# The mixing stage of a two-layer network in another static order, and the transposed attention weights copied by ScalarE (two banks) and VectorE (one)

## The chip, the cores and the metric

One Trainium2 chip, one of its cores. The engines are TensorE (PE: matrix products and transposes), VectorE (DVE), ScalarE (ACT), GpSimd (POOL) and SyncE (SP, which issues most of the transfers). The metric is the device time of one execution, in microseconds; the kernel before is told by the median of its runs.

## The reference

Two layers over a sequence of 256 tokens of width 1024, all in float32. Each layer is a feed-forward block, a token-mixing block, a cross-attention to a memory of 256 tokens, and a second feed-forward block, each with a norm before and after. The token mixing projects the input to 2032 columns and feeds four mixers side by side:

```python
def _token_mixing(u, w_in, ...):
    proj = u @ w_in
    p_mla, p_nsa, p_fox, p_s5 = jnp.split(proj, ...)
    o_mla = _mla(...)      # causal attention over low-rank projections
    o_nsa = _nsa(...)      # compressed + selected + window attention, gated
    o_fox = _fox(...)      # causal attention with a forget gate
    o_s5 = _s5(...)        # state-space scan
    y = jnp.stack([o_mla, o_nsa, o_fox, o_s5], axis=2)
    y = _rmsnorm(y, group_g).reshape(B, S, MIX_WIDTH)
    return y @ w_out
```

The compressed branch of `_nsa` runs blocks of 32 keys and values through a small network (phi: 2048 to 256 to 64). The cross-attention needs keys and values of the normalized memory, `mem_n @ w_kv`, which depend on nothing in the layer.

## The kernel before

**Weights.** Each large weight is cut into units of 1 MB (128 x 2048). SyncE loads them one after the other into three slots; a load waits until the slot's former unit has been split by VectorE (L454). ScalarE copies the unit, in two halves, to a rounded high part (L666), VectorE subtracts it for the low part (L1141, called by `split_mid`). Products take three matmuls, high x high, high x low, low x high (`three`, L1677). ScalarE may overwrite a slot's high part when TensorE has done with the unit of three before (`unit_done`).

**The order of the work** is written out by hand, once for each engine; every engine runs its list in order and waits on semaphores. Between the two feed-forward blocks there are units 0 to 7 (input projection; 3 groups of two half units besides the first two), 8 and 9 (memory keys, `kv_half(0..1)`), 10 to 13 (phi), 14 to 19 (memory keys and values, `kv_half(2..7)`), 20 to 23 (output projection) and those of the cross-attention. The memory products fill TensorE's time between the steps of the mixers. Each has two halves of 24 matmuls of 256 columns; they go to PSUM banks 1, 1, 1, 3, 0, 1, 0, 1, emptied by ScalarE (`evac_kv`, L949 and L951). A half unit of the input projection (`group_half`) is 12 matmuls of 512 columns.

**Attention.** Four groups in the order 0 (MLA), 3 (fox), 1 and 2 (selected and window), each of four steps on TensorE: `scores` (16 matmuls), `probs_transposed` (12 transposes to banks 5, 6 and 7, L2002), `times_values` (24 matmuls). Between them VectorE takes the maximum (`attention_max`, L1430 and L1431), ScalarE the exponentials (`attention`, L932 and L935), then both copy the transposed weights from PSUM to SBUF: ScalarE bank 5 (L941), VectorE banks 6 and 7 (L1442). VectorE divides by the sum (`attention_out`, L1449).

**Steps around the change.** VectorE rotates the queries and keys of the second mixer together (L1404 to L1417). The memory tiles are made from a transposed copy in `zone`: x_hi by ScalarE (L966), x_lo by VectorE (`mem_lo`), in the order two tiles, `attention_max(0)`, six tiles. ScalarE has exponential, logarithm (L973) and tanh (L976), for which it loads function tables. The mixer outputs are normalized by group (`group_norm`), transposed (`mixer_transposed`, L2208), split into high and low (`mixer_hi`, L1053, `mixer_lo`) and multiplied with units 20 to 23 (`unit_rows`), whose sums lie in banks 0 to 3.

```python
                def attention_t(g):
                    act.wait_ge(*E.at("att_t", POS[g] + 1))
                    a.activation(probs_t[:, 0:512], bank(5), ACT.Copy).then_inc(sem["att_tc_act"], 1)
                def attention_copy(g):
                    dve.wait_ge(*E.at("att_t", POS[g] + 1))
                    v.tensor_copy(probs_t[:, 512:1536], bank(6, 2)).then_inc(sem["att_tc_dve"], 1)
```

## Time and profile before

| | us |
|---|---|
| median of 3 runs | 1329.68 (1329.3 to 1329.98) |
| the profiled execution | 1331.46 |
| its span | 1329.7 |
| TensorE, VectorE, ScalarE busy in it | 1284.1, 845.5, 683.3 |
| TensorE's mean granted clock | 0.983 |

Busy time is an average over stages. What matters is which engine the chain that ended last runs through, and, on that engine, where it stands still (the brackets behind a row of the timeline: how long it was idle and what released it) and where its clock is granted in part only (PEclk: 1.00 is 2.4 GHz, 0.50 is 1.2 GHz).

### The profile page before, as it was taken

The page shows a single profiled execution, that of the slowest core. Times are in us where ns is not written, and L with a number is a line of the kernel's source. Part 1 is how long each engine was busy: PE and PEld are TensorE (multiplying, and loading weights), DVE is VectorE, ACT ScalarE, POOL GpSimd, SP SyncE. Part 2 cuts the span into 40 slices and gives each one's busy share as a digit, 9 for nine tenths or more (in the row PEclk, how much of TensorE's full clock was granted, in tenths as well). Part 3 has the DMA queues.
Part 4 walks back from the last instruction along what each step waited for, and adds up shares of the span by engine and source line. Part 5 has one row for each costly group of instructions (what it writes and reads, how often), then busy time and mean ns, then how long its engine had stood idle before and what let it go on. Part 6 is the DMA issues. An engine that isn't in the chain of part 4 may idle for free.

```text
span 1329.7 us, 18613 instructions
## 1 busy us (share of the span) xinstructions
PE 1284.1 (97%) x6836; PEld 1096.8 (82%) x6836; DVE 845.5 (64%) x1173; ACT 683.3 (51%) x1113; POOL 235.8 (18%) x250
## 2 busy tenths in 40 slices
PE   7999999988999999999999999999899999999998
PEld 5887888778998978888878878887789888788886
DVE  5657857675666665555576577666766665755554
ACT  6455446474455554444464544554655454644443
POOL 1628900000002010000045296000000020100000
PEclk9999999998999999999999999999889999999999
DMA  9654543324334246555455555534143343555551
GB/s 345 247 189 158 204 175 127 142 96 159 127 127 167 102 170 247 189 189 189 158 181 188 188 185 189 190 112 158 64 159 127 128 171 112 215 188 189 189 189 64
DMA packets 32442, 222.65 MB, mean 167 GB/s; under 512 B 3584, under 2 KB 4096, under 8 KB 6784
## 3 DMA queue, kind: packets, MB, share of 16 engines
q1 hardware_dynamic: 30080, 209.28, 43.9%
q10 hardware_dynamic: 2304, 12.58, 2.5%
q8 instruction: 38, 0.62, 0.2%
q14 instruction: 20, 0.16, 0.0%
HBM read 219.75 MB, written 2.10 MB: 167 GB/s over the span
## 4 chain that ended last, share of the span: by engine, by line
PE 83%; DVE 7%; ACT 4%; issue 3%; DMA 1%; SPq 0%; POOL 0%; DVEq 0%; ACTq 0%; POOLq 0%
PE PS L1675 80%; DVE w_lo L1141 3%; PE PS L1790 1%; ACT w_hi L666 1%; DMA raw<-in_weights 1%; DVE x_lo L1144 1%; PE PS L2002 1%; ACT work L960 1%; DVE work L1144 0%; DVE work L1141 0%; DVE PS L1141 0%; DVE rope_t L1312 0%; ACT x_hi L714 0%; DVE h L1144 0%; DVE zone L1141 0%
## 5 line engine op out<-in xcount | busy, mean ns | idle before, releaser
L1141 DVE TENSOR_TENSOR w_lo<-raw,w_hi 128x1024 fp32r<-128x1024 f32 (+1 forms) x394 | 503.1, 1320 | 231.9 <-ACT w_hi L666 228.9
L666 ACT ACTIVATE w_hi<-raw 128x1024 fp32r<-128x1024 f32 x384 | 384.7, 1053 | 241.4 <-PE PS L1675 239.2
L1675 PE MATMUL PS<-w_hi,x_hi 128*128 128x512 f32 (+2 forms) x1104 | 426.9, 387 | 10.6 <-DVE x_lo L1144 5.3
L1675 PE MATMUL PS<-w_lo,x_hi 128*128 128x512 f32 (+2 forms) x1104 | 415.8, 377 | 0.0
L1675 PE MATMUL PS<-w_hi,x_lo 128*128 128x512 f32 (+2 forms) x1104 | 410.4, 378 | 0.0
L1675 PEld LDWEIGHTS PS<-w_hi,x_hi 128*128 128x128 f32 x1104 | 210.5, 191 | 53.2 <-DVE w_lo L1141 7.8
L1675 PEld LDWEIGHTS PS<-w_hi,x_lo 128*128 128x128 f32 x1104 | 210.0, 190 | 38.4
L1675 PEld LDWEIGHTS PS<-w_lo,x_hi 128*128 128x128 f32 x1104 | 211.0, 191 | 35.2 <-issue 0.5
L1675 PE MATMUL PS<-w_hi,hid_hi 128*128 128x512 f32 (+1 forms) x368 | 141.2, 386 | 0.0
L1675 PE MATMUL PS<-w_lo,hid_hi 128*128 128x512 f32 (+1 forms) x368 | 140.4, 385 | 0.0
L516 POOL TENSOR_SCALAR st<-st 128x1 f32<-128x1 f32 x32 | 20.3, 634 | 631.7 <-ACT proj L689 562.3
L727 ACT ACTIVATE work<-PS,st 128x256 f32<-128x256 f32 x88 | 41.8, 475 | 149.3 <-PE PS L1675 147.7
L1675 PE MATMUL PS<-w_hi,hid_lo 128*128 128x512 f32 (+1 forms) x368 | 111.2, 380 | 0.0
L1675 PE MATMUL PS<-x_hi,w_hi 128*128 128x256 f32 x288 | 87.9, 305 | 14.7 <-DVE x_lo L1144 7.0
L1675 PE MATMUL PS<-x_lo,w_hi 128*128 128x256 f32 x288 | 84.6, 294 | 0.0
L1675 PE MATMUL PS<-x_hi,w_lo 128*128 128x256 f32 x288 | 84.3, 293 | 0.0
L1144 DVE SCALAR_TENSOR_TENSOR work<-work,PS 128x256 f32<-128x256 f32 x88 | 36.7, 417 | 71.6 <-ACT work L727 71.6
L1675 PEld LDWEIGHTS PS<-w_hi,hid_hi 128*128 128x128 f32 (+1 forms) x368 | 67.3, 183 | 14.0
L1675 PEld LDWEIGHTS PS<-w_lo,hid_hi 128*128 128x128 f32 (+1 forms) x368 | 66.8, 182 | 13.6
L1675 PEld LDWEIGHTS PS<-w_hi,hid_lo 128*128 128x128 f32 (+1 forms) x368 | 66.5, 181 | 13.8
L1675 PEld LDWEIGHTS PS<-x_hi,w_hi 128*128 128x128 f32 x288 | 58.4, 203 | 17.8 <-issue 8.7
L1675 PEld LDWEIGHTS PS<-x_lo,w_hi 128*128 128x128 f32 x288 | 58.7, 204 | 0.1
(275 smaller groups left out, 1342.1 us busy)
## 6 DMA issues: line engine op xcount, KB each, us to landing
raw<-in_weights SPq DMA_DIRECT2D x194, 1024.0 KB, 4.7
pmat<-in_mats ACTq DMA_DIRECT2D x3, 1664.0 KB, 8.0
...
```

What stands on the lines that cost most here:

```text
L516: E.step(g.tensor_scalar(o, a, s1, s2, op0, op1))
L666: a.activation(w_hi[s][:, c_], raw[s][:, c_], ACT.Copy).then_inc(sem[hi_done[s]], 1)
L727: a.activation(f_th[:, t], bank(4 + t)[:, 0:UC], ACT.Tanh, scale=rstd[n][:, t:t + 1]).then_inc(sem["tanh_done"], 1)
L960: i = a.activation(y_to[32 * q:32 * q + 32, :, :, r], g_from[32 * r:32 * r + 32, q], ACT.Copy, scale=0.5)
L1141: return v.tensor_tensor(o, x_, y_, op)
L1144: return v.scalar_tensor_tensor(out=o, in0=x_, scalar=s_, in1=y_, op0=op0, op1=op1)
L1675: return t_.matmul(o, a_, b_, start=first, stop=last)
L1790: o = t_.transpose(bank(6)[:, j * S + t * P:j * S + (t + 1) * P], f_hid[:, t, j * P:(j + 1) * P], ident)
L2002: i = t_.transpose(bank(b)[:, hh * P:(hh + 1) * P], probs[:, at:at + P], ident)
```

## The change

The units between the input projection and the output projection are loaded in another order: keys and values 8, 9, 10, 12, 14, 15, 17, 19, phi 11, 13, 16, 18. All key/value units but the first go to bank 1. The lists of TensorE, ScalarE and VectorE are written anew: half of group (2,1) before the MLA transposes; scores of group 0 before the last half unit; the memory's x_hi in two halves, each when TensorE has done with the input tiles in the same place, and all x_lo before the maximum of group 0; the two rotations apart, that of the queries later; the compressed branch later; the output projection by token tile (`out_rows`), mixed with the last attention group and the compressed branch. ScalarE copies banks 5 and 6 of the transposed weights, VectorE bank 7. VectorE makes the key copy that ScalarE made (L982). The variance of the MLA norm is put before the second scan.

```diff
              [(I_FK, I_FV), (I_FV, I_FF)]]
 N_IN = 2 * len(IN_GROUPS)
 
-M_PHI = N_IN + 2
-KV_UNITS = [N_IN, N_IN + 1, *range(M_PHI + 4, M_PHI + 10)]
-KV_BANK = [1, 1, 1, 3, 0, 1, 0, 1]
-M_OUT = M_PHI + 10
+PHI_UNITS = [N_IN + i for i in (3, 5, 8, 10)]
+KV_UNITS = [N_IN + i for i in (0, 1, 2, 4, 6, 7, 9, 11)]
+KV_BANK = [0] + 7 * [1]
+M_OUT = N_IN + 12
 M_Q = M_OUT + 4
 M_O = M_Q + 4
 N_MID = M_O + 4
@@ -221,7 +221,7 @@
...
                 def attention_t(g):
                     act.wait_ge(*E.at("att_t", POS[g] + 1))
-                    a.activation(probs_t[:, 0:512], bank(5), ACT.Copy).then_inc(sem["att_tc_act"], 1)
+                    a.activation(probs_t[:, 0:1024], bank(5, 2), ACT.Copy).then_inc(sem["att_tc_act"], 1)
...
                 i.then_inc(sem["s5_sc_act"], 1)
+                act.wait_ge(*E.at("mem_in", 16))
+                for half in range(2):
+                    s, n, _ = mid(l, N_IN - 2 + half)
+                    act.wait_ge(*E.at(unit_done[s], n + 1))
+                    mem_hi(range(half * KT // 2, (half + 1) * KT // 2))
                 evac(3, 1)
-                act.wait_ge(*E.at("mem_in", 16))
-                for k in range(KT):
-                    a.activation(xh3[:, k], zone[:, 2048 + k * S:2048 + (k + 1) * S], ACT.Copy,
-                                     scale=pcol[:, C_MEM + k:C_MEM + k + 1]).then_inc(sem["x_hi_done"], 1)
-                attention(0)
-
-                act.wait_ge(*E.at("fox_x", 1))
-                a.activation(f_b2, f_a, ACT.Exp).then_inc(sem["fox_e"], 1)
-                act.wait_ge(*E.at("fox_e", 1))
-                a.activation(f_a, f_b2, ACT.Ln, bias=1.0).then_inc(sem["fox_ln"], 1)
+                split_mid(9)
...
-                act.wait_ge(*E.at("nsa_t", 1))
-                a.activation(kc2[0:HD, :], bank(6)[0:HD], ACT.Copy).then_inc(sem["nsa_kc"], 1)
-                a.activation(nsa_q[0:HD, :], bank(2, 2)[0:HD], ACT.Copy).then_inc(sem["nsa_tc_act"], 1)
+                attention(0)
+
+                act.wait_ge(*E.at("fox_x", 1))
+                a.activation(f_b2, f_a, ACT.Exp).then_inc(sem["fox_e"], 1)
+                act.wait_ge(*E.at("fox_e", 1))
+                a.activation(f_a, f_b2, ACT.Ln, bias=1.0).then_inc(sem["fox_ln"], 1)
                 split_mid(10)
+                evac_kv(0)
+                attention_t(0)
...
                 split_mid(11)
-                split_mid(13)
                 evac_kv(1)
+                split_mid(12)
                 act.wait_ge(*E.at("fox_cum", 1))
                 for hh in range(H):
                     i = a.activation(ka[HD:HD + 1, hh], bank(5)[32 * hh:32 * hh + 1, 0:S], ACT.Copy,
                                      scale=-1.0 / SCALE[3])
                 i.then_inc(sem["fox_nc"], 1)
+                evac_kv(2)
                 act.wait_ge(*E.at("fox_tq", 1))
                 a.activation(qk_a[0:HD, 0:H * S], bank(6, 2)[0:HD], ACT.Copy).then_inc(sem["fox_qt"], 1)
-                split_mid(12)
+                split_mid(13)
                 split_mid(14)
+                evac_kv(3)
                 attention(3)
 
                 split_mid(15)
-                evac_kv(2)
                 attention_t(3)
                 split_mid(16)
+                evac_kv(4)
+                split_mid(17)
+                act.wait_ge(*E.at("nsa_t", 2))
+                a.activation(nsa_q[0:HD, :], bank(6, 2)[0:HD], ACT.Copy).then_inc(sem["nsa_tc_act"], 1)
+                evac_kv(5)
+                attention(1)
+
+                split_mid(18)
+                attention_t(1)
+                split_mid(19)
+                evac_kv(6)
+                group_squares((0, 2), "att_out", 2)
+                split_mid(20)
+                act.wait_ge(*E.at("phi_h", 1))
+                act.wait_ge(*E.at("s5_out", 1))
+                for k in range(2):
+                    a.activation(s5_tiles[0][:, k], s_out[:, k], ACT.Copy).then_inc(sem["x_hi_done"], 1)
+                split_mid(21)
...
                 for n_ in range(2):
                     act.wait_ge(*E.at("grp_t", n_ + 1))
                     mixer_hi(MO_ORDER[2 * n_ + 2:2 * n_ + 4])
-                group_squares((1,), 4)
+                attention(2)
+                act.wait_ge(*E.at("cmp_x", 1))
+                a.activation(cp, cp, ACT.Exp).then_inc(sem["cmp_e"], 1)
+                attention_t(2)
+                act.wait_ge(*E.at("cmp_t", 1))
+                a.activation(probs_t[0:NC_CMP, 0:1024], bank(6, 2)[0:NC_CMP], ACT.Copy).then_inc(sem["cmp_tc"], 1)
+                group_squares((1,), "cmp_done", 1)
                 split_mid(23)
...
-                E.step(v.tensor_tensor_scan(s_tmp[3], kc2[:, :], s_tmp[2], 0.0, ALU.mult, ALU.add))
                 dve.wait_ge(*E.at("mla_sq", 1))
                 variance([(ss[N_MLA][:, 0:2], MLA_Q), (ss[N_MLA][:, 2:4], MLA_KV)])
+                E.step(v.tensor_tensor_scan(s_tmp[3], kc2[:, :], s_tmp[2], 0.0, ALU.mult, ALU.add))
...
                 def attention_copy(g):
                     dve.wait_ge(*E.at("att_t", POS[g] + 1))
-                    v.tensor_copy(probs_t[:, 512:1536], bank(6, 2)).then_inc(sem["att_tc_dve"], 1)
+                    v.tensor_copy(probs_t[:, 1024:1536], bank(7)).then_inc(sem["att_tc_dve"], 1)
...
+                mem_lo(range(KT))
                 attention_max(0)
-                mem_lo(range(2, KT))
                 split_mid(9)
...
-                attention_copy(0)
-
+                split_mid(10)
+                E.step(v.memset(zone[:, 7168:7168 + TT * P], 0.0))
+                dve.wait_ge(*E.at("fox_ln", 1))
+                tt(lf[:, :, 0:P:32], flog, f_a, ALU.subtract).then_inc(sem["fox_lf"], 1)
                 dve.wait_ge(*E.at("gate_th", 1))
                 E.step(v.tensor_scalar(gates, gates, 0.5, 0.5, ALU.mult, ALU.add))
 
                 attention_out(0)
                 split_mid(11)
-                split_mid(13)
+                split_mid(12)
...
                 dve.wait_ge(*E.at("fox_tk", 1))
                 v.tensor_copy(qk_a[0:HD, H * S:], bank(2, 2)[0:HD]).then_inc(sem["fox_kt"], 1)
-                split_mid(12)
                 dve.wait_ge(*E.at("s5_rstd_all", 1))
                 for k in range(2):
-                    i = stt(s_out[:, k], s_out[:, k], pcol[:, C_GRP + 6 + k:C_GRP + 7 + k], bank(1)[:, 0:S],
+                    i = stt(s_out[:, k], s_out[:, k], pcol[:, C_GRP + 6 + k:C_GRP + 7 + k], bank(4)[:, 0:S],
                             ALU.mult, ALU.mult)
                 i.then_inc(sem["s5_out"], 1)
+                dve.wait_ge(*E.at("proj_done", 7))
+                dve.wait_ge(*E.at("nsa_rope", 1))
+                nsa_rope(v3(pr3[:, :, I_NQ:I_KC], "p t (h d) -> p t h d", d=HD), H)
+                split_mid(13)
                 split_mid(14)
                 dve.wait_ge(*E.at("s5_var", 1))
                 attention_max(3)
 
                 split_mid(15)
                 attention_copy(3)
-                s, n, _ = mid(l, M_PHI + 3)
+                split_mid(16)
+                attention_out(3)
+                split_mid(17)
+                attention_max(1)
+
+                split_mid(18)
+                attention_copy(1)
+                split_mid(19)
+                s, n, _ = mid(l, PHI_UNITS[3])
                 dve.wait_ge(*E.at(unit_done[s], n + 1))
                 v.tensor_copy(phi_rows[0:2 * NC_CMP], bank(0)[0:2 * NC_CMP]).then_inc(sem["phi_h"], 1)
-                split_mid(16)
+                dve.wait_ge(*E.at("grp_sq", 1))
+                variance([(grp(ss, 0, 3, 2), 256)])
+                split_mid(20)
+                group_norm(0, 0, 3, 2)
+                dve.wait_ge(*E.at("x_hi_done", FILL[FI_MO] + 2))
+                for k in range(2):
+                    tt(s5_tiles[1][:, k], s_out[:, k], s5_tiles[0][:, k].bitcast(F32), ALU.subtract).then_inc(sem["x_split"], 1)
+                split_mid(21)
+                attention_out(1)
...
-                attention_out(3)
                 dve.wait_ge(*E.at("phi_th", 1))
                 stt(hx, hx2, 1.0, hx, ALU.add, ALU.mult).then_inc(sem["phi_hid"], 1)
-                split_mid(17)
...
+                split_mid(22)
+                attention_max(2)
+                mixer_lo(1)
+                mixer_lo(2)
...
-                group(3, 1)
+                group_half(3, 1, 0)
...
+                def out_rows(q, t, js):
+
+                    s, _, ns = mid(l, M_OUT + q)
+                    pe.wait_ge(*E.at(split_done[s], ns + 1))
+                    pe.wait_ge(*E.at("x_split", FILL[FI_MO] + 2 * q + 2))
+                    c_ = slice(t * P, (t + 1) * P)
+                    for j in js:
+                        ah, al = (x_[:, j, c_] for x_ in s5_tiles) if q == 0 else \
+                            (x_[:, MO_ORDER[2 * q + j], c_] for x_ in (xh3, xl3))
+                        o = [y_ps[:, t, n_ * 512:(n_ + 1) * 512] for n_ in range(2)]
+                        wh, wl = ([w[s][:, j * D + n_ * 512:j * D + (n_ + 1) * 512] for n_ in range(2)] for w in (w_hi, w_lo))
+                        for n_ in range(2):
+                            mm(o[n_], ah, wh[n_], q == 0 and j == 0, False)
+                            mm(o[n_], ah, wl[n_], False, False)
+                        for n_ in range(2):
+                            i = mm(o[n_], al, wh[n_], False, False)
+                    if t == 1 and j == 1:
+                        i.then_inc(sem[unit_done[s]], 1)
+
+                pe.wait_ge(*E.at("mla_qt", 1))
+                pe.wait_ge(*E.at("mla_kt", 1))
+                pe.wait_ge(*E.at("s5_yc", 1))
+                scores(0)
+                group_half(3, 1, 1)
+                pe.wait_ge(*E.at("proj_done", 8))
                 kv_half(0, 0)
...
                 kv_half(0, 1)
+                pe.wait_ge(*E.at("proj_done", 9))
+                kv_half(1, 0)
 
                 pe.wait_ge(s_con, 16)
                 pe.wait_ge(*E.at("s5_zt", 1))
                 pe.wait_ge(s_con, 16)
-                pe.wait_ge(*E.at("nsa_tc_act", 1))
-                pe.wait_ge(s_con, 16)
                 pe.wait_ge(*E.at("nsa_tc_dve", 1))
                 probs_transposed(0)
-                pe.wait_ge(*E.at("xkv_done", 1))
-                kv_half(1, 0)
+                kv_half(1, 1)
                 times_values(0)
-                pe.wait_ge(*E.at("blocks_done", 2))
-                phi_unit(M_PHI)
...
+                pe.wait_ge(*E.at("xkv_done", 2))
+                kv_half(2, 0)
+                pe.wait_ge(*E.at("blocks_done", 2))
+                pe.wait_ge(*E.at("xkv_done", 1))
+                phi_unit(0)
+                kv_half(2, 1)
 
                 fox_heads(I_FQ, 6, "fox_tq")
                 pe.wait_ge(s_con, 16)
                 pe.wait_ge(*E.at("att_out", 1))
                 fox_heads(I_FK, 2, "fox_tk")
-                phi_unit(M_PHI + 1)
-
                 pe.wait_ge(*E.at("s5_rstd", 1))
-                pe.wait_ge(*E.at("xkv_done", 2))
                 for t in range(TT):
-                    i = mm(bank(1)[:, t * P:(t + 1) * P], s5_r[:, t:t + 1].to_broadcast([P, P]), ident, True, True)
+                    i = mm(bank(4)[:, t * P:(t + 1) * P], s5_r[:, t:t + 1].to_broadcast([P, P]), ident, True, True)
...
+                pe.wait_ge(*E.at("xkv_done", 3))
+                kv_half(3, 0)
                 pe.wait_ge(*E.at("fox_one", 1))
                 pe.wait_ge(*E.at("fox_nc", 1))
                 pe.wait_ge(*E.at("fox_qt", 1))
                 pe.wait_ge(*E.at("fox_kt", 1))
+                pe.wait_ge(*E.at("s5_out", 1))
                 scores(3)
-
-                pe.wait_ge(*E.at("s5_out", 1))
-                kv_half(2, 0)
-                phi_unit(M_PHI + 2)
-                kv_half(2, 1)
+                kv_half(3, 1)
+                phi_unit(1)
+                pe.wait_ge(*E.at("xkv_done", 4))
+                kv_half(4, 0)
                 probs_transposed(3)
-                phi_unit(M_PHI + 3)
-                pe.wait_ge(*E.at("att_exp", 2))
-                kv_half(3, 0)
+                kv_half(4, 1)
                 times_values(3)
+                pe.wait_ge(s_con, 16)
+                pe.wait_ge(*E.at("nsa_rope", 2))
...
+                i.then_inc(sem["nsa_t"], 1)
+                pe.wait_ge(*E.at("xkv_done", 5))
+                kv_half(5, 0)
+                pe.wait_ge(*E.at("att_out", 2))
+                pe.wait_ge(*E.at("nsa_tc_act", 1))
+                scores(1)
+                kv_half(5, 1)
+                phi_unit(2)
+                pe.wait_ge(*E.at("xkv_done", 6))
+                kv_half(6, 0)
+                probs_transposed(1)
+                kv_half(6, 1)
+                phi_unit(3)
+                pe.wait_ge(*E.at("xkv_done", 7))
+                kv_half(7, 0)
+                pe.wait_ge(*E.at("nsa_v", 1))
+                times_values(1)
...
-                kv_half(3, 1)
-
+                kv_half(7, 1)
+                pe.wait_ge(*E.at("att_out", 3))
+                scores(2)
...
+
+                pe.wait_ge(s_con, 16)
+                pe.wait_ge(*E.at("grp_xn", 1))
+                mixer_transposed(MO_ORDER[2:4])
+                mixer_transposed(MO_ORDER[4:6])
+                pe.wait_ge(*E.at("xkv_done", 8))
+                out_rows(0, 0, range(2))
                 pe.wait_ge(*E.at("phi_c", 1))
...
+                out_rows(1, 0, range(2))
                 pe.wait_ge(s_con, 16)
                 pe.wait_ge(*E.at("cmp_x", 1))
-                probs_transposed(1)
-                kv_half(5, 1)
-                pe.wait_ge(*E.at("nsa_v", 1))
-                times_values(1)
+                pe.wait_ge(*E.at("x_split", FILL[FI_MO] + 6))
+                probs_transposed(2)
+                out_rows(0, 1, range(2))
+                times_values(2)
...
+                out_rows(1, 1, range(2))
+                pe.wait_ge(*E.at("att_out", 4))
                 pe.wait_ge(*E.at("cmp_tc", 1))
...
+                out_rows(2, 0, range(2))
+                out_rows(2, 1, [0])
                 pe.wait_ge(s_con, 16)
-                pe.wait_ge(*E.at("cmp_done", 1))
...
+                pe.wait_ge(*E.at("grp_xn", 2))
+                mixer_transposed(MO_ORDER[6:8])
+                out_rows(2, 1, [1])
+                s, _, ns = mid(l, M_OUT + 3)
+                pe.wait_ge(*E.at("x_split", FILL[FI_MO] + KT))
+                unit_rows(s, ns, [(xh3[:, k], xl3[:, k]) for k in MO_ORDER[6:8]], False, True)
                 pe.wait_ge(*E.at("x_split", FILL[FI_MO] + KT))
                 rows_transposed(2)
 
@@ -2340,13 +2350,17 @@
             u = u.reshape(KT, P, 2 * UC).transpose(1, 0, 2)
```

## Rows read from the trace of the kernel before

**Rows 1.** The page, part 1: busy us (share of the span) and instructions.

```profile
PE 1284.1 (97%) x6836; PEld 1096.8 (82%) x6836; DVE 845.5 (64%) x1173; ACT 683.3 (51%) x1113; POOL 235.8 (18%) x250
```

**Rows 2.** The page, part 4: the chain that ended last, by engine.

```profile
PE 83%; DVE 7%; ACT 4%; issue 3%; DMA 1%; SPq 0%; POOL 0%; DVEq 0%; ACTq 0%; POOLq 0%
```

**Rows 3.** Windows: stretch, length, busy us (instructions) by engine; PEclk; DMA share; GB/s.

```profile
247.30:413.80 166.50, 156.22 (x1039) 142.01 (x1039) 106.66 (x186) 86.23 (x162) 6.15 (x9) 0.94 0.35 127
...
902.60:1069.10 166.50, 156.23 (x1038) 142.06 (x1039) 106.65 (x186) 86.22 (x162) 6.15 (x9) 0.94 0.35 127
...
250.00:255.00 5.00, 5.00 (x19) 4.00 (x17) 4.15 (x10) 1.34 (x4) 0.00 (x0) 0.66 0.10 11
...
288.60:292.00 3.40, 3.40 (x17) 3.40 (x18) 3.40 (x7) 3.38 (x10) 0.00 (x0) 0.55 0.00 0
...
304.00:310.00 6.00, 6.00 (x42) 5.26 (x41) 3.33 (x7) 0.55 (x1) 0.00 (x0) 0.72 0.01 3
...
324.30:330.00 5.70, 5.70 (x30) 5.59 (x31) 3.21 (x6) 2.35 (x8) 0.00 (x0) 0.57 0.99 417
...
380.00:384.00 4.00, 4.00 (x24) 4.00 (x23) 2.62 (x5) 3.12 (x9) 0.00 (x0) 0.57 0.00 0
```

**Rows 4.** Timeline of PE, first layer: start, us, line, operation, count [idle before <-releaser].

```profile
242.12 0.40 PE L1675 MATMUL PS<-w_hi,x_lo 128*128 128x512 f32 x1
...
242.35 0.40 PE L1675 MATMUL PS<-w_hi,x_hi 128*128 128x512 f32 x1
...
249.64 0.40 PE L1953 MATMUL PS<-con,proj 128*96 128x128 f32 x2 [2.33 <-DVE proj L1141]
...
257.40 4.47 PE L1675 MATMUL PS<-pmat,nsa_q 96*128 96x384 f32 x12
...
288.60 0.58 PE L1675 MATMUL PS<-x_hi,w_hi 128*128 128x256 f32 x1 [3.02 <-DVE x_lo L1144]
...
299.07 0.38 PE L1675 MATMUL PS<-x_hi,w_hi 128*128 128x256 f32 x1 [0.78 <-ACT zone L949]
...
303.11 1.08 PE L1675 MATMUL PS<-v_mla,zone 128*128 128x65 f32 x8 [0.91 <-DVE zone L1442]
...
318.48 2.78 PE L1675 MATMUL PS<-qk_a 65*128 65x256 f32 x16
...
324.29 0.55 PE L1675 MATMUL PS<-x_hi,w_hi 128*128 128x256 f32 x1 [3.03 <-DVE w_lo L1141]
```

**Rows 5.** Timeline of DVE, first layer, same columns.

```profile
278.69 1.29 DVE L1141 TENSOR_TENSOR rope_t<-proj,con 128x512 f32<-128x512 f32 x2
...
280.02 0.76 DVE L1141 TENSOR_TENSOR proj<-rope_t 128x256 f32<-128x256 f32 x2
...
301.75 1.22 DVE L1442 COPY zone<-PS 128x1024 f32<-128x1024 f32 x1
...
316.89 1.21 DVE L1511 COPY qk_a<-PS 64x1024 f32<-64x1024 f32 x1
...
318.73 2.36 DVE L1141 TENSOR_TENSOR w_lo<-raw,w_hi 128x1024 fp32r<-128x1024 f32 x2 [0.63 <-ACT w_hi L666]
...
321.01 0.87 DVE L1144 SCALAR_TENSOR_TENSOR work<-work,pcol,PS 128x256 f32<-128x256 f32 x2
...
324.06 1.29 DVE L1141 TENSOR_TENSOR PS<-PS,con 128x512 f32<-128x512 f32 x2
```

**Rows 6.** Timeline of ACT, first layer and its FFN.

```profile
164.82 1.28 ACT L666 ACT_TABLE_LOAD   x1 [3.13 <-PE PS L1675]
...
295.05 1.01 ACT L983 ACTIVATE nsa_q<-PS 64x1024 f32<-64x1024 f32 x1
...
298.91 0.59 ACT L941 ACTIVATE zone<-PS 128x512 f32<-128x512 f32 x1
...
327.65 1.57 ACT L932 ACTIVATE zone<-PS,st 128x256 f32<-128x256 f32 x4 [6.11 <-DVE st L1141]
...
329.09 1.16 ACT L935 ACTIVATE zone<-PS,st 128x128 f32<-128x128 f32 x4
```

238 lines of the change are left out of this document (75 added, 163 removed).

## The prediction

> **What bounds the kernel now.** First the page: TensorE is busy 97% of the span, VectorE 64%, ScalarE 51% [rows 1], and the chain that ended last runs through TensorE for 83% [rows 2]. The change adds and removes no matrix work, so it can only touch the time in which TensorE stands still or runs at a lower clock between the third input group and the end of the output projection. I took that stretch from 247.3 us, where TensorE has ended group (2,0) and both orders still agree, to 413.8 us, the end of the last output unit. Of its 166.5 us TensorE is busy 156.2, so it waits 10.3, at a mean granted clock of 0.94; the second layer repeats it from 902.6 to 1069.1 with the same figures [rows 3]. Then the timeline, for where it waits: 2.33 us before the MLA transposes, 3.02 in the first key/value unit, 0.78 before the second, 0.91 before the first times-values, 3.03 before unit 14 [rows 4]; with 0.2 us of crumbs that is the 10.3. Last, windows behind each wait: the granted clock is 0.66 over 5 us, 0.55 over 3.4, 0.72 over 6, 0.57 over 5.7, and, with no wait ahead of it, 0.57 over 4 us at 380 [rows 3]. A share lost is one minus the clock, times the stretch: 1.70 + 1.53 + 1.68 + 2.45 + 1.72 = 9.1 us. **Losses are 10.3 + 9.1 = 19.4 us a layer**, 38.8 in all; without them the stretch is 147.1 us. That is what the change can win, and what new losses are counted against.
>
> **The unit costs.** A half unit of 512 columns is 12 matmuls, 0.23 us apart [rows 4]: 2.75 us. A half of a key/value unit is 24 matmuls, from 299.07 to 302.20 (303.11 less 0.91), of which some 0.2 is a tail that the next block overlaps: 2.9 us, 0.12 each [rows 4]. A phi unit is 16 such matmuls, 1.9 us. Scores are 2.8 us [rows 4]. VectorE's half of a weight split is 2.36 us for a unit [rows 5], ScalarE's two copies come ahead of it.
>
> **Part 1, the MLA transposes.** Before, they start at 249.64 after 2.33 us of waiting for VectorE's normalized projection, the clock is low behind it, and the MLA projections start at 257.40 [rows 4]. Afterwards the first half of group (2,1) is put in the gap: 247.3 + 2.75 = 250.05, by then the projection is there; transposes 0.6, second half 2.75, so the projections start at 253.4. Gain 4.0 us, which is 2.33 + 1.70. That VectorE computes the variance ahead of the second scan brings nothing by itself: the scan and the products still stand ahead of the normalization on its queue.
>
> **Part 2, memory tiles.** Before, six of eight x_lo tiles stand behind the softmax maximum of group 0 on VectorE, and TensorE waits 3.02 us for them [rows 4]. Afterwards ScalarE makes four x_hi tiles while TensorE does scores(0) and the last half unit (2.8 + 2.75 us), the other four when that half unit ends, VectorE follows tile by tile, and the maximum comes after all of them. TensorE starts tiles 0 to 3 at once (1.45 us of work) and meets the fifth some 0.4 us too early. Gain 3.0 + 1.5 less 0.4.
>
> **Part 3, group 0's probabilities.** The waits of 0.78 (one evacuation) and 0.91 (VectorE's copy) [rows 4] go: between the transposes and times_values stands a key/value half of 2.9 us, and the copy is shared anew. ScalarE now copies two banks, 1.01 us instead of 0.59 [rows 6]; VectorE one, about 0.7 instead of 1.22 [rows 5] (an estimate: half the columns and the fixed part). The two run side by side, so the pair is ready 0.2 us sooner, and 2.9 us of key/value matmuls or output rows cover it each time: this half of the change I cost at nothing; without the cover it would bring 0.2 us, four times a layer. Over a layer VectorE saves 2.1 us and ScalarE takes 1.7. Gain of the part 1.7 + 1.7 of clock.
>
> **Part 4, the order of units.** Before, the four phi units (1.9 us each on TensorE) come nearly in a row, while each needs 2.36 us of VectorE: TensorE outruns the splits and waits 3.03 us at unit 14 [rows 4, 5], with 2.45 us of low clock behind [rows 3]. Afterwards they are units 11, 13, 16, 18 with key/value units of 5.8 us between, and splits are taken in the order of loading. A slot's load follows the split of three units before, so the one issue that was early (13 ahead of 12) goes too; SyncE's queue has as many loads as before, merely of other units. Gain 3.0 + 2.45.
>
> **What comes new.** (a) Fox attention. Count from the end of the key transposes. VectorE: copy of the keys 1.21, s5 output 0.87, rotation of four heads 1.29 + 0.76, which was moved here, splits 13 and 14, 4.72, the maximum 324.06 to 327.65, 3.6: 12.5 us [rows 5, 6]. ScalarE then takes 2.6 for the exponentials (1.57 + 1.16, overlapping) [rows 6], and 1.28 for a table load, for now the last function before it is the logarithm: a load comes behind the wait, not under it, as the one at 164.82 that follows 3.13 us of waiting shows [rows 6]. Sum 16.3. TensorE from the same moment: 0.5 broadcast, key/value half 2.9, scores 2.8, half 2.9, phi 1.9, half 2.9: 13.9. It waits 2.4 us at probs_transposed(3), and the clock falls after it as after the others, 1.5 us. What stands behind is unit 14's second half and times_values. (b) In the output rows, the first mixer tiles' x_lo stand on VectorE behind split 22 and the maximum of group 2. From ScalarE's phi tanh: evacuation 0.6, first half of the split 1.0, then VectorE's 2.36, maximum 3.4, two tiles 0.87: 8.2 us [rows 5, 6]. TensorE over the same: the last 1.7 of scores(2), 0.7 of phi products, 0.9 of transposes, a half output unit 2.75, compressed scores 1.7: 7.7. Wait 0.5, behind it the probabilities of group 2. (c) The last unit needs the tiles of the group that is normed last: addition, squares, variance, GpSimd's power and the norm, some 3.3 us with their hand-overs, split 23 of 2.36 and two tiles of 0.87 make 6.6, against 5.9 of output rows and transposes: 0.7 us. The short operations in (b) and (c) are estimates after rows of like size, good to a microsecond either way. (d) The fall at 380 has no wait ahead of it, only scores and small products of 64 and 15 rows; such a stretch is still there (scores, phi output, transposes), so I keep one such fall, 1.7 us. (e) ScalarE waits about 6 us for unit 10 with the fox query copy and splits 13 and 14 behind it; the copy is still 1 us ahead of scores(3), so this costs nothing, and microsecond for microsecond beyond that.
>
> New losses: 0.4 + 2.4 + 0.5 + 0.7 + 1.5 + 1.7 = 7.2, with crumbs of 0.1 us 7.3. **Gain 19.4 - 7.3 = 12.1 us a layer, 24.2 in all.** The profiled execution took 1331.46 us (its span is 1329.7) and lies 1.8 above the median, so 1307.3 for it and 1305.5 for the median.
>
> For the two unseen sizes the bounds are: a new table load costs between nothing (hidden, or placed elsewhere) and 1.28 plus 1.5 of clock; I take it in full, since it sits on the longer path. A fall of the clock costs 0 to 2.45 us [rows 3], and there may be none or three.
>
> Where the load stands is the compiler's choice. Before, a load comes at the logarithm and, since a tanh follows, another at once, so no row shows what an exponential behind a logarithm needs; I place it at the first function of another kind, the exponentials of (a). The Trainium skill (ScalarE: Activation LUTs, Table sets) says otherwise: one shipped set has both the logarithm and the exponential, so that the one behind the other needs no second load. By that the sum would be the one of the rival "load elsewhere" below, 1302.5, and not 1305.5.
>
> **Rivals.** *Load elsewhere.* The exponentials need no load, and it comes ahead of the phi tanh, on the path to the compressed scores. In (a) 16.3 - 1.28 - 13.9 = 1.1 us of waiting stay, in (b) 0.5 + 1.28 = 1.8: the same sum in two shorter waits. After 0.78 us the clock kept its level, after 0.91 it fell [rows 3, 4]; if it keeps it here, 1.5 us a layer are saved: 1302.5. For it speaks the page named above, against it nothing but that no row shows it.
> *More places fall.* The new order has many seams with 1 us to spare, and ledger (d) may hold more than one fall. Two further falls (3.4) and waits of 2.5 us a layer halve the gain: 1317. For: five falls in 166 us before, one without a cause that I can name. Against: the three largest waits go surely.
> *All hidden.* The load is off the path and nothing falls without a wait: losses 2.8 us a layer, 1296.5. Against: VectorE's 12.5 us in (a) are counted from rows.
> *Slower: bank 1.* All key/value units but the first now use one bank, where three were used before, so each must wait until ScalarE has emptied it for the last. The one such wait before cost 0.78 [rows 4]; with a fall of 1.5 us behind each, six hand-overs cost 13.7 us a layer, more than the 12.1, and the kernel takes 1333. It decides from the point at which ScalarE reaches the evacuation later than TensorE the next unit. Against: between any two units stand a phi unit, transposes or times_values, 1.9 us or more, for a copy of 0.6; only at unit 19 is ScalarE busy ahead (a copy and a split), and has still 1.2 us.
> *No change.* The lists move work, but the waits that end last could come back in full elsewhere, 12 us of them; the stage behind depends on TensorE's end alone, so nothing swallows a gain there. 1329.7.
>
> **How the numbers follow.** The forecast 0.42, load elsewhere 0.2, more falls 0.2, all hidden 0.1, no change 0.03, bank 1 0.05. The range takes in the first four and somewhat over: 1295 to 1318. About 0.2% is what a measurement of this kernel can tell from no change; above it faster 0.92, same 0.03, slower 0.05.
>
> **What would show it.** Right: no wait before the MLA transposes; no wait over 0.6 us in the first key/value unit; none for w_lo in the middle; one wait of 1 to 2.5 us at the fox transposes of line 2002's operation, released by ScalarE; one or two low windows a layer instead of five; the stretch near 154 us. Wrong: waits of key/value units for ScalarE's evacuation, low clock in more than three places, or a stretch of over 160 us.

## The result, and the profile after

The changed kernel takes **1297.6 us** (median of 4 runs, 1297.27 to 1299.1) against 1329.83 beside it: ratio 0.9759 [0.9742, 0.9776], 32 us. The forecast was 1305.5 in a range from 1295 to 1318: the direction was right and so were the waits that go, the gain was a third larger than worked out, and the case that came nearest is the rival "all hidden" (1296.5), to which the prediction gave 0.1.

The profiled execution took 1297.27 us, its span is 1295.4, 34.3 less than before. Its page, parts 1 and 4 (the same lines as [rows 1, 2]):

```profile
PE 1266.7 (98%) x6836; PEld 1082.3 (84%) x6836; DVE 840.3 (65%) x1175; ACT 683.7 (53%) x1111; POOL 236.7 (18%) x250
...
PE 87%; DVE 6%; issue 3%; ACT 2%; DMA 1%; POOL 1%; SPq 0%; DVEq 0%; POOLq 0%; ACTq 0%
```

TensorE does the same 6836 instructions and is busy 17.4 us less, because it is not slowed. The rest of the gain is waiting. Windows after: the two stretches that answer to the first two of [rows 3], then four of the times of layer 1 at which the clock was low before (other work stands there now).

```profile
247.30:396.90 149.60, 147.36 (x1039) 133.92 (x1038) 104.06 (x187) 86.36 (x161) 5.46 (x8) 1.00 0.39 139
885.90:1035.50 149.60, 147.72 (x1040) 134.38 (x1039) 104.28 (x187) 86.48 (x162) 5.29 (x8) 1.00 0.40 141
250.00:255.00 5.00, 5.00 (x24) 3.73 (x22) 4.90 (x10) 3.81 (x7) 0.00 (x0) 1.00 0.07 18
...
288.60:292.00 3.40, 3.40 (x32) 3.40 (x31) 3.08 (x7) 2.91 (x5) 0.00 (x0) 1.00 0.45 188
304.00:310.00 6.00, 6.00 (x54) 6.00 (x53) 1.88 (x3) 3.35 (x4) 0.00 (x0) 1.00 0.46 188
324.30:330.00 5.70, 5.70 (x52) 5.70 (x52) 4.72 (x6) 5.53 (x7) 0.00 (x0) 1.00 0.52 172
```

The stretch was 166.5 us and is 149.6: 16.9 less, twice over 33.8 of the 34.3 us of span. TensorE now waits 149.60 - 147.36 = 2.24 us in it where it waited 10.3, and the clock column is 1.00 in both layers. So in layer 1 8.0 us came from waits and 8.9 from the clock, by which TensorE's busy time fell from 156.22 to 147.36; in layer 2 it was 8.4 and 8.5. (The windows of [rows 3] put the clock at 9.1, a little more than it cost.) **A good half of the gain is TensorE's clock**. Its timeline after, for the seams (the places where one block of work ends and TensorE may have to wait for the next) of [rows 4]:

```profile
249.73 0.38 PE L1951 MATMUL PS<-con,proj 128*96 128x128 f32 x2
...
253.14 4.47 PE L1671 MATMUL PS<-pmat,nsa_q 96*128 96x384 f32 x12
...
278.18 0.28 PE L1671 MATMUL PS<-x_hi,w_hi 128*128 128x256 f32 x1
...
322.90 1.50 PE L2000 MATMUL PS<-con,zone 128*128 128x128 f32 x12 [1.30 <-ACT zone L933]
...
367.07 1.95 PE L1671 MATMUL PS<-rope_t,nsa_q 64*128 64x15 f32 x16
...
391.29 0.50 PE L1671 MATMUL PS<-w_hi,x_hi 128*128 128x512 f32 x1 [0.94 <-DVE x_lo L1146]
```

No bracket stands behind the MLA transposes (249.73), the first key/value unit (278.18) or the compressed scores (367.07). Two waits are left: 1.30 us at the fox transposes, released by ScalarE's exponentials, and 0.94 for the last unit's x_lo (in layer 2 it is 0.6). What stands ahead of the first, on VectorE and then on ScalarE:

```profile
308.12 1.22 DVE L1517 COPY qk_a<-PS 64x1024 f32<-64x1024 f32 x1 [5.50 <-PE PS L2050]
309.26 0.85 DVE L1146 SCALAR_TENSOR_TENSOR work<-work,pcol,PS 128x256 f32<-128x256 f32 x2
310.04 1.28 DVE L1143 TENSOR_TENSOR rope_t<-proj,con 128x512 f32<-128x512 f32 x2
311.36 0.76 DVE L1143 TENSOR_TENSOR proj<-rope_t 128x256 f32<-128x256 f32 x2
312.03 4.62 DVE L1143 TENSOR_TENSOR w_lo<-raw,w_hi 128x1024 fp32r<-128x1024 f32 x4
316.57 1.29 DVE L1143 TENSOR_TENSOR PS<-PS,con 128x512 f32<-128x512 f32 x2
...
319.95 0.17 DVE L1143 TENSOR_TENSOR st<-st 128x8 f32<-128x8 f32 x1
```

```profile
316.93 0.60 ACT L947 ACTIVATE zone<-PS 128x512 f32<-128x512 f32 x1 [4.87 <-PE PS L1671]
317.54 1.28 ACT L930 ACT_TABLE_LOAD   x1
320.16 1.57 ACT L930 ACTIVATE zone<-PS,st 128x256 f32<-128x256 f32 x4 [1.33 <-DVE st L1143]
321.60 1.16 ACT L933 ACTIVATE zone<-PS,st 128x128 f32<-128x128 f32 x4
```

VectorE is 12.0 us from the key copy to the last small operation (12.5 forecast), the exponentials 2.6 (2.6 forecast). The table load is where the prediction put it, at the exponentials behind the logarithm, but it ran at 317.54, **while** ScalarE was still waiting for the maximum: the 1.33 us in the bracket come after the load, and its 1.28 us cost nothing.

Of the signs that the prediction named, these came: no wait before the MLA transposes, none in the first key/value unit, none for w_lo in the middle, and one of 1.30 us at the fox transposes. Two did not: there is no low window at all where one or two were expected, and the stretch is 149.6 us and not 154.

### The profile page after: what moved, and what is told of

Its sections match the earlier page's. It is cut to its first block, busy times and chain, and to the rows that moved or that the text cites. A ratio compares the mean times of both kernels' runs of the same rounds, so it can differ in the third digit from the quotient of the medians.

```text
span 1295.4 us, 18623 instructions
## 1 busy us (share of the span) xinstructions
PE 1266.7 (98%) x6836; PEld 1082.3 (84%) x6836; DVE 840.3 (65%) x1175; ACT 683.7 (53%) x1111; POOL 236.7 (18%) x250
## 4 chain that ended last, share of the span: by engine, by line
PE 87%; DVE 6%; issue 3%; ACT 2%; DMA 1%; POOL 1%; SPq 0%; DVEq 0%; POOLq 0%; ACTq 0%
PE PS L1671 82%; DVE w_lo L1143 3%; PE PS L1786 1%; DMA raw<-in_weights 1%; PE PS L2000 1%; DVE x_lo L1146 1%; DVE work L1146 0%; ACT w_hi L666 0%; DVE PS L1143 0%; DVE rope_t L1314 0%; ACT x_hi L714 0%; DVE h L1146 0%; PE PS L1812 0%; PE PS L2050 0%; PE PS L2259 0%
## 5 line engine op out<-in xcount | busy, mean ns | idle before, releaser
L1671 PE MATMUL PS<-x_hi,w_hi 128*128 128x256 f32 x288 | 84.0, 292 | 1.0 <-DVE x_lo L1146 0.9
L1671 PE MATMUL PS<-x_lo,w_hi 128*128 128x256 f32 x288 | 81.4, 283 | 0.0
L1671 PE MATMUL PS<-x_hi,w_lo 128*128 128x256 f32 x288 | 81.4, 283 | 0.0
L1671 PEld LDWEIGHTS PS<-w_hi,hid_lo 128*128 128x128 f32 (+1 forms) x368 | 66.5, 181 | 13.9
L1671 PEld LDWEIGHTS PS<-w_hi,hid_hi 128*128 128x128 f32 (+1 forms) x368 | 66.5, 181 | 13.6
L1671 PEld LDWEIGHTS PS<-x_hi,w_hi 128*128 128x128 f32 x288 | 55.0, 191 | 2.4 <-issue 1.8
L1671 PEld LDWEIGHTS PS<-x_lo,w_hi 128*128 128x128 f32 x288 | 55.1, 191 | 0.1
```

Source lines behind the costliest of these rows:

```text
L1671: return t_.matmul(o, a_, b_, start=first, stop=last)
```

## The experiments

Two families: kernels a... are the changed kernel with one thing undone, moved or added, kernels b... are the kernel before with one part of the change, or nothing, put in. Times stand beside the kernel before on the same chip: 1330.82 us for a1 to a4, 1330.12 for b1 to b4, 1330.86 for a5 to a7 and b5. Theory, as on record in the prediction: the gain is the waits and the low clock of the four parts, the sharing of the copies is worth nothing.

### a1: the sharing of the copies undone

```diff
-a.activation(probs_t[:, 0:1024], bank(5, 2), ACT.Copy)...
+a.activation(probs_t[:, 0:512], bank(5), ACT.Copy)...
-v.tensor_copy(probs_t[:, 1024:1536], bank(7))...
+v.tensor_copy(probs_t[:, 512:1536], bank(6, 2))...
```

> The kernel after, with the sharing of the transposed weights undone: ScalarE copies bank 5 (0.6 us), VectorE banks 6 and 7 (1.22 us). My theory: every copy lies under 2.9 us of key/value matmuls or output rows, so it changes nothing: 1297.6 within 0.15% (1295.7 to 1299.5), and no new wait of TensorE before times_values. Rival: VectorE's queue is what the wait at the fox transposes hangs on, and 0.5 us more on it for each group moves later steps: up to 0.5 us for each of four groups in two layers, 1301.6.

Measured: 1298.21 us (1297.45 to 1298.44), ratio 0.9762 [0.9743, 0.9782]; the waits are the same two, 1.3 and 0.9. The sharing of the copies, which the title names, makes 0.6 us between the medians, which the runs can't tell from nothing. The pieces are as costed: ScalarE's two banks take 1.03 us where one took 0.59, VectorE's one takes 0.68 where two took 1.22, and 2.9 us of matmuls cover either.

### a2: a second wait ahead of the load

```diff
 act.wait_ge(*E.at("att_max", POS[g] + 1))
+act.wait_ge(*E.at("att_s", POS[g] + 1))
```

> The kernel after, with a second wait (already met) between the wait for the maximum and the first exponential of every group. Theory A: a wait that stands alone next to an activation is carried by the activation itself, so the table load in front of it runs while ScalarE waits; with two waits the load comes behind the first, as in the loop of the feed-forward block (wait, load, activation). Then the load falls on the path: the exponentials start 1.3 us later, TensorE's wait at the fox transposes grows from 1.30 to 2.6 us, and the time by 2.6 us to 1300.2; if the clock falls behind the longer wait, by another 1.5 us a layer, 1303.2. Rival B: the load's place does not hang on the waits: no change, 1297.6.

Measured: 1297.99 us (1296.62 to 1302.24), ratio 0.9767 [0.9739, 0.9795]. ScalarE's timeline of a2:

```profile
318.93 1.28 ACT L931 ACT_TABLE_LOAD   x1
321.54 1.57 ACT L931 ACTIVATE zone<-PS,st 128x256 f32<-128x256 f32 x4 [1.33 <-DVE st L1144]
```

The load still ran ahead of both waits and TensorE's wait was still 1.3: the edit did not do what it was made for, and the theory that a second wait ahead of the exponentials puts the load behind the first fell. What does put it there is shown by a6.

### a3: part 1 undone

```diff
-                group_half(2, 1, 0)
...
-                group_half(2, 1, 1)
+                group(2, 1)
```

> The kernel after, with part 1 undone: the whole group (2,1) after the MLA transposes. Theory: the wait of 2.33 us comes back in each layer, and with it the low clock over some 3.4 us (1.7): 4.0 us a layer, 1305.6. Rival: slack behind it (VectorE, ScalarE ahead of the later steps) takes up part of the shift, under 2.3 us a layer, below 1302.2. Rival 2: the wait comes back but the clock holds, as it did behind 1.30 us in the kernel after: 4.7 us in all, 1302.3.

Measured: 1304.92 us (1303.76 to 1306.55), ratio 0.9815 [0.9794, 0.9837], 7.3 more than the changed kernel. TensorE's timeline of a3, and its windows behind the wait in both layers:

```profile
248.73 0.40 PE L1949 MATMUL PS<-con,proj 128*96 128x128 f32 x2 [2.27 <-DVE proj L1143]
```

```profile
248.00:254.00 6.00, 5.27 (x20) 4.32 (x21) 5.24 (x12) 1.26 (x4) 0.00 (x0) 0.72 0.03 5
889.50:895.50 6.00, 4.24 (x15) 3.64 (x16) 5.93 (x11) 1.56 (x5) 0.83 (x2) 0.72 0.00 0
```

Wait and fall are both back, 2.3 + 6 x 0.28 = 1.7 in each layer: 8.0 us by this count for the 7.3 measured. Part 1 is settled, at the 4.0 a layer that it was given less a little.

### b1: part 1 alone, in the kernel before

```diff
                 group(2, 0)
+                group_half(2, 1, 0)
...
-                group(2, 1)
+                group_half(2, 1, 1)
```

> The kernel before with part 1 alone: the first half of group (2,1) ahead of the MLA transposes. Theory: 2.33 us of waiting and 1.7 of low clock go in each layer, and what follows moves with it: 1329.8 - 8.0 = 1321.8. Rival: the later steps wait for ScalarE and VectorE, and less than half arrives at the end: over 1325.8.

Measured: 1322.82 us (1322.23 to 1324.35), ratio 0.9951 [0.9933, 0.997]: 7.3 us less, the same amount from the other side. The waits of 3.0, 3.0 and 0.9 stay, and that of 0.78 shrinks to 0.4. Windows of b1, all the low ones of the first mixer:

```profile
282.00:290.00 8.00, 5.78 (x27) 5.49 (x28) 6.83 (x13) 6.51 (x15) 0.00 (x0) 0.57 0.10 15
316.00:324.00 8.00, 4.97 (x25) 4.87 (x24) 6.38 (x10) 1.89 (x6) 0.00 (x0) 0.57 0.87 340
374.00:380.00 6.00, 6.00 (x38) 5.93 (x38) 4.16 (x6) 4.29 (x10) 0.00 (x0) 0.72 0.01 3
```

The fall behind the removed wait is gone and so is the one that stood at 304, but those behind the two waits of 3.0 are longer than before, and the mean granted clock of b1's runs is 0.984 to 0.987 (before: mostly 0.983 and 0.984). Waits explain some 5.3 of the 7.3 us, so the clock gave back about 2 and not the 3.4 that the theory had.

### b2: part 2 alone

```diff
-                mem_lo(range(2))
+                mem_lo(range(KT))
                 attention_max(0)
-                mem_lo(range(2, KT))
```

> The kernel before with part 2 alone, in its simplest form: all eight x_lo tiles ahead of the maximum of group 0. Theory: the wait of 3.02 us shrinks to under 0.5 and the low clock behind it goes, but the maximum, the exponentials and all that hangs on them come 2.5 us later, and TensorE waits for them at the transposes of group 0 instead: part of the 4.5 us a layer comes back, 1322 to 1328. Rival: nothing is lost behind, 1320.8.

Measured: 1334.95 us (1332.28 to 1337.27), ratio 1.0046 [1.003, 1.0063]: **slower** by 0.3 to 0.6%, which neither theory had. TensorE's timeline of b2:

```profile
291.53 1.89 PE L2071 MATMUL PS<-con,proj 128*64 128x128 f32 x8 [5.47 <-ACT st L971]
```

The 3.02 us wait of the key/value unit is gone, and 5.5 us stand in front of the transposes of the second mixer's queries. These write to banks 2 and 3, where scores(0) lie until the exponentials have read them, and those follow the maximum, which six tiles now hold up. The changed kernel escapes this because it makes those transposes much later and in other banks. Part 2 is not a gain by itself but one half of a pair.

### a7: part 2 undone, in the changed kernel

```diff
-                mem_lo(range(KT))
+                mem_lo(range(2))
                 attention_max(0)
+                mem_lo(range(2, KT))
```

> The changed kernel with VectorE's old order of the memory tiles: two tiles, attention_max(0), then the other six, everything else as in the changed kernel. Theory (making all eight ahead of the maxima is what took away the 3.02 us wait of the first key and value unit): that unit, which starts at 278.2 us without a wait, needs the third tile only after the 3.4 us of the maxima, so TensorE waits 2 to 3 us in each layer: 1297.6 + 2 x 2.5 = 1302.6 us, plus 0 to 1.5 a layer for a clock fall, 1301 to 1306. Rival (in the new order the tiles are early enough anyway, because the work ahead of them shrank): no wait, 1297.6 us.

Measured: 1303.86 us (1301.94 to 1305.54), ratio 0.98 [0.9786, 0.9813], 6.3 more. TensorE's timeline of a7, and its windows behind the wait in layer 1 and in layer 2:

```profile
281.73 0.39 PE L1672 MATMUL PS<-x_hi,w_hi 128*128 128x256 f32 x1 [1.74 <-DVE x_lo L1146]
```

```profile
282.00:286.00 4.00, 4.00 (x21) 3.92 (x21) 3.92 (x7) 1.64 (x2) 0.00 (x0) 0.57 0.01 4
919.00:925.00 6.00, 4.26 (x26) 3.66 (x25) 5.87 (x13) 4.99 (x12) 0.63 (x1) 1.00 0.00 0
```

The wait is back behind the second tile, 1.7 us in each layer: shorter than the 2 to 3 of the expectation, but the rival (tiles early enough anyway) fell. In layer 1 a fall of 4 x 0.43 = 1.7 us follows it, in layer 2 none does. Same wait, same program, two outcomes. The waits and the fall make 5.1 of the 6.3 us; 0.9 more lie ahead of the mixer, since TensorE reaches the unit at 279.11 in this profile and at 278.18 in that of the changed kernel. The other 0.3 us are not assigned.

### b3: a phi unit ahead of the key/value half

```diff
+                phi_unit(M_PHI + 2)
                 pe.wait_ge(*E.at("s5_out", 1))
                 kv_half(2, 0)
-                phi_unit(M_PHI + 2)
```

> The kernel before with one swap on TensorE: the third phi unit (12), whose split is done by then, ahead of the first half of unit 14. Theory: the wait of 3.03 us is the ring of three slots - unit 14 may only be split when phi unit 11 is through, and between them TensorE has 3.3 us of work where the split takes 6.8 - so 1.9 us of it are filled, about 1.1 us stay, and the low clock of 2.45 us behind it goes or shrinks: 1329.8 - 3.8 - (0 to 4.9) = 1321 to 1326. Rival: the phi unit itself must wait as long: 1329.8.

Measured: 1317.68 us (1315.74 to 1324.16), ratio 0.9926 [0.99, 0.9951], 12.4 us less than before, more than either theory gave. The wait for unit 14 went from 3.03 to 1.1 us, while two others grew (to 1.2 and 0.5), so waits explain some 2 us. The rest is the clock. Windows of b3, with the five stretches of [rows 3] and the only low one of both mixers:

```profile
250.00:255.00 5.00, 5.00 (x24) 4.12 (x23) 4.73 (x10) 3.21 (x5) 0.00 (x0) 1.00 0.18 28
288.60:292.00 3.40, 3.40 (x32) 3.39 (x31) 3.19 (x5) 3.34 (x6) 0.00 (x0) 1.00 0.22 34
...
895.00:901.00 6.00, 4.66 (x17) 4.01 (x18) 5.82 (x13) 1.19 (x3) 0.92 (x2) 0.72 0.00 0
```

The waits of 2.4 and 3.0 us before 250 and 288 are there, and the clock did not fall behind them in layer 1. The edit comes after both. Yet it can hardly be chance alone: the mean granted clock of b3's six runs is 0.998 three times (1315.7 to 1316.2 us), 0.994 once (1319.2) and 0.988 twice (1322.8 and 1324.2), while the 18 runs of the kernel before on the same chip have 0.981 to 0.990. So the 12.4 us are a median over runs with and without most of the falls, the two at 0.988 are those that fit the expectation of 1321 to 1326, and how an edit can act on a stretch ahead of it stays **open**.

### b4: the fall at 380

```diff
+                pe.wait_ge(*E.at("xkv_done", 6))
+                kv_half(7, 0)
                 ...
-                pe.wait_ge(*E.at("xkv_done", 6))
-                kv_half(7, 0)
```

> The kernel before with the first half of unit 19 between the scores of group 2 and the small products of the compressed branch, which stood back to back (2.9 and 2.0 us, 64 and 15 rows) just ahead of the clock's fall at 380 us that no wait explains. Theory A: the two together make a stretch thin enough for the clock to fall; apart they do not, the clock stays at 1.00 there and 1.7 us a layer are saved: 1326.4. Theory B: the fall depends on when the stretch comes, not on what it is; it stays or moves: 1329.8.

Measured: 1326.94 us (10 runs, 1324.3 to 1331.66), ratio 0.9984 [0.9965, 1.0003]. Windows of b4:

```profile
250.00:255.00 5.00, 5.00 (x26) 4.13 (x24) 4.71 (x10) 3.05 (x5) 0.00 (x0) 1.00 0.05 13
286.00:294.00 8.00, 7.15 (x39) 6.84 (x40) 5.78 (x13) 6.75 (x16) 0.00 (x0) 0.59 0.24 70
304.00:310.00 6.00, 6.00 (x55) 5.75 (x55) 4.68 (x9) 2.00 (x2) 0.00 (x0) 1.00 0.10 14
...
380.00:384.00 4.00, 4.00 (x35) 4.00 (x36) 3.92 (x4) 3.51 (x7) 0.00 (x0) 1.00 0.00 0
```

The fall at 380 is gone in both layers, but so are those at 250 and 304, which lie before the edit, while the one at 288 is longer. The time can't be told from no change. Of the kernels that leave that place as it was, b1, b2 and b5 have the fall in both layers (at 374 to 380 and 380 to 386 in layer 1) and b3 in neither. So whether the moved half is what kept the clock stays **open**.

### b5: the kernel before, again

> The kernel before, unchanged, profiled a second time. Theory (the waits of TensorE are the program's, the places where its clock falls are partly the execution's): the waits are the same to 0.1 us (2.3, 3.0, 3.0, 0.9, 0.8), the falls are as many in all but not all in the same places. Rival (the falls are the program's too): the same five places in both layers, with the same depths.

Measured: 1331.91 us, one run. TensorE's waits are the same to 0.1 us. Windows of b5, the stretch and three places of [rows 3]:

```profile
247.30:413.80 166.50, 156.29 (x1039) 141.85 (x1038) 106.70 (x186) 86.19 (x162) 6.66 (x9) 0.94 0.36 127
```

```profile
250.00:255.00 5.00, 4.86 (x18) 3.99 (x19) 4.66 (x10) 1.19 (x3) 0.00 (x0) 0.66 0.00 0
288.60:292.00 3.40, 2.94 (x13) 2.94 (x14) 3.40 (x8) 3.33 (x10) 0.00 (x0) 0.53 0.00 0
304.00:310.00 6.00, 6.00 (x42) 5.23 (x41) 2.97 (x7) 0.10 (x1) 0.00 (x0) 0.72 0.02 3
```

These two profiles bear the rival out: ten falls in the same ten places, with about the same depths. But both are executions with a mean clock of 0.983, as 19 of the 34 runs of this kernel that stand beside the experiments. The others have 0.981 (1334.7 us) to 0.990 (1325.9 us), so executions of the same unchanged program do differ in their low clock, by as much as 9 us; where, no trace shows. One more trace of the commonest kind can't refute my theory, which stays **open**. That falls can differ for the same stretch of instructions is also shown by b2, b3 and b4: the clock is 1.00 at 250 to 255 in all three, ahead of their edits and behind the same wait of 2.4 us.

### a6: the load really behind the wait

```diff
 act.wait_ge(*E.at("att_max", POS[g] + 1))
+if g == 3:
+    a.activation(probe, nb[:, 0:1], ACT.Copy)
```

> The changed kernel with a Copy of one column on ScalarE between the wait for attention_max(3) and the exponentials of attention(3), its result used by nothing, so that the table load of 1.28 us in front of the first Exp has the wait ahead of it, as the prediction assumed. Theory (the changed kernel hides the load under the wait because the load is issued ahead of an activation that carries the wait itself): the Copy ends at about 320.4 us, the load runs to 321.8, the exps end 1.5 us later than before, TensorE's wait at the fox transposes grows from 1.3 to 2.8 us a layer, and the time from 1297.6 to about 1300.6 us; a fall of the clock behind the longer wait would add 0 to 1.5 a layer, up to 1303.6. Rival (the load is hidden in any place): wait 1.3 to 1.5 and time 1297.6 to 1298.

Measured: 1303.3 us (1301.92 to 1306.4), ratio 0.98 [0.9786, 0.9814], 5.7 more than the changed kernel. ScalarE's timeline of a6, then TensorE's wait and the windows behind it in both layers:

```profile
320.24 0.20 ACT L931 ACTIVATE st<-st 128x1 f32<-128x1 f32 x1 [2.63 <-DVE st L1146]
320.44 1.28 ACT L933 ACT_TABLE_LOAD   x1
321.74 1.57 ACT L933 ACTIVATE zone<-PS,st 128x256 f32<-128x256 f32 x4
```

```profile
324.48 0.87 PE L2003 MATMUL PS<-con,zone 128*128 128x128 f32 x3 [2.80 <-ACT zone L936]
```

```profile
322.00:330.00 8.00, 5.52 (x36) 5.55 (x37) 3.65 (x4) 6.92 (x13) 0.00 (x0) 0.79 0.16 41
963.00:971.00 8.00, 5.20 (x33) 5.23 (x33) 3.33 (x4) 6.90 (x14) 0.00 (x0) 0.79 0.13 25
```

This is the experiment that settles the first of the misses. With a Copy of one column between the wait and the exponentials, the load runs behind the wait, TensorE's wait is 2.8 us instead of 1.3, and the clock falls behind it in both layers, by 8 x 0.21 = 1.7 us. That would be 1.5 + 1.7 = 3.2 us a layer; the start of the last output unit (391.29 and 1029.35 in the changed kernel, 394.24 and 1035.34 here) moves by 3.0 a layer, so the fall cost some 1.5. Measured are 5.7 in all. Term (a) of the prediction was 2.4 of wait and 1.5 of fall: for that term this kernel is the one that was predicted.

### a4 and a5: the two waits that are left

a4 takes the rotation of the queries ahead of the copy of the fox keys, into the 5.5 us in which VectorE waits for them. a5 is a4 and, besides, takes split 23 ahead of the compressed branch's last steps:

```diff
+                dve.wait_ge(*E.at("proj_done", 7))
+                dve.wait_ge(*E.at("nsa_rope", 1))
+                nsa_rope(v3(pr3[:, :, I_NQ:I_KC], ...), H)
                 dve.wait_ge(*E.at("fox_tk", 1))
...
-                nsa_rope(v3(pr3[:, :, I_NQ:I_KC], ...), H)
                 split_mid(13)
```

```diff
                 attention_t(2)
+                split_mid(23)
...
                 group_squares((1,), "cmp_done", 1)
-                split_mid(23)
...
+                split_mid(23)
                 attention_out(2)
...
                 group_norm(1, 1, 2)
-                split_mid(23)
```

> The kernel after, with the rotation of the queries (2.05 us of VectorE) moved ahead of the copy of the fox keys, into 5.5 us in which VectorE waits. Theory: the remaining wait of 1.30 us at the fox transposes hangs on VectorE's queue of key copy, s5 output, rotation, two splits and maximum; without the rotation it is gone, 1.3 us a layer, 1295.0. Rival: the splits wait for ScalarE then, so the maximum moves by less, and the wait stays over 0.6 us: 1296.3 or more.

> The changed kernel with the queries' rotation moved ahead of the keys' copy (as in the earlier run that took the wait at the fox transposes away, 1295.5 us) and, in addition, the split of the last but two unit (23) moved earlier: on ScalarE after attention_t(2), on VectorE before attention_out(2). Theory (the 0.94 us wait of TensorE for x_lo at the last output unit is VectorE's work in row, so work taken out of its way shortens it): both remaining waits shrink, 1.3 and some 0.6 to 0.9 a layer, total near 1297.6 - 2.6 - 1.0 = 1294 us, and no wait above 0.5 us in TensorE's list of waits of the mixer. Rival (the wait has another bound, the evacuation of the compressed attention's output before it): the 0.9 us stays or moves to the groups' transposes, and the time equals the 1295.5 us of the rotation alone.

Measured: a4 1295.53 us (1294.92 to 1301.13), ratio 0.9757 [0.9727, 0.9786]; a5 **1294.14 us** (1293.86 to 1297.35), ratio 0.9731 [0.9717, 0.9744], the fastest of all. In a4 the wait at the fox transposes is gone, in both layers; its interval overlaps that of the changed kernel, so by time alone the gain of 2.1 us is not shown. TensorE's only wait in a5's first mixer (in all, times, longest):

```profile
PE PS L1671 <- DVE x_lo L1146: 0.4, 1, 0.4
```

Of the mixer's 2.24 us, 0.4 are left. The rival for a5 (the last wait bound by something else) fell by the trace; by time the two kernels' medians lie 1.4 us apart and their intervals overlap.

## Why the prediction was right, and where it was off

**What bounds, and the four parts: held.** Losses of 19.4 us a layer and a floor of 147.1 were the right frame: after the change TensorE is busy 147.36 us at full clock. Part 1 was tested from both sides (7.3 us each time, 8.0 forecast). Part 2's wait comes back when it is undone, with a fall in one layer of two (6.3 us; 8.2 forecast), but the part only pays beside the later transposes (b2), which the prediction did not see as a condition. Part 3's sharing is worth nothing that the runs could see (a1), as costed; its two waits of 0.78 and 0.91 are gone, and no run undid the part. Part 4 was only tried in the kernel before, by b3, where a shorter wait came with more clock than the wait explains; its 3.0 us of wait are gone in the changed kernel, and no run undid it alone there. So of the 32 us some 13.6 are shown by undoing (a3, a7); the rest is read from the waits and clocks of the two traces.

**What comes new: five terms too large.** 7.3 us a layer forecast, 2.24 measured. Two rows of ScalarE's timeline in the trace of before, on which the first term turns:

```profile
0.73 1.28 ACT L786 ACT_TABLE_LOAD   x1 [0.73 <-PEq L2407]
2.95 0.20 ACT L786 ACTIVATE st<-con 128x1 f32<-128x1 f32 x1 [0.93 <-DMA con<-in_consts]
```

Term by term:

- *Table load, 1.28 of the 2.4 in (a).* The step that failed is the sentence "a load comes behind the wait, not under it", taken from the row at 164.82 [rows 6]. At the exponentials the load went ahead of the wait (after: 317.54; a2: 318.93). The two rows above show that the trace of before had this case too: ScalarE's very first load ran while its activation waited for the constants, and 0.93 us of that wait were left when the load had ended. The prediction took one row for a rule where the trace had both cases. The row at 164.82 is in a loop over units, whose waits compare with a register's value, while the other two waits are on constants; that this is what makes the difference is argued and not tested. Without the load (a) is 16.3 - 1.28 - 13.9 = 1.1 us; 1.30 was measured. The Trainium skill (ScalarE: Activation LUTs, Table sets) would have had no load at all behind the logarithm; the trace disagrees, since one stands there, of 1.28 us.
- *The fall behind (a), 1.5.* None came behind 1.30 us, one came behind 2.80 in both layers (a6). The term fits a wait of that length, and was wrong with it.
- *(d), a fall without a wait, 1.7.* None came. The small products now stand between output rows: 382.19 in the trace after is followed by full matmuls at once. I called its cause unknown and kept it; b4 left it unknown. So why this term, the largest of the five, came to nothing is open.
- *0.4 for the fifth x_lo tile, 0.5 for (b).* Neither came. In (b) ScalarE and VectorE take from the phi tanh (360.50) to the second tile (368.6) 8.1 us, as forecast (8.2), but TensorE's own work to the end of the compressed scores (367.07 and 1.95, with 0.1 of overlap) is 8.4 rather than 7.7.
- *(c), 0.7:* 0.94 and, in layer 2, 0.6.

With 0.1 of crumbs, the sum of these differences is 5.1 us a layer, 10.1 in all, and 24.2 + 10.1 is the 34.3 by which the span shrank (33.8 of it in the two stretches; layer 2 waits 1.88 us and not 2.24, and the floor is 0.3 above the 147.1). 3.2 of the 5.1 are falls of the clock; 1.1 is (a)'s wait, the load of 1.28 less the 0.2 by which the rest of (a) came out longer.

**The rivals.** "All hidden" put losses at 2.8 a layer with VectorE's 12.5 us standing; it came out at 2.24. It deserved more than 0.1, since two of the things that it needs, the load off the path and no fall behind (a), are one event. The third, no fall (d), is another, and no run gives a reason for it: that the time came so near to this rival is in part luck. "Bank 1" needed key/value units that wait for ScalarE's evacuation: there is no such wait in the trace after. "Load elsewhere" had the wait right (1.1) and the reason wrong.
